# Three products of 256 columns for the feed-forward gate and up, two operands placed 64 bytes on, rotary angles in the middle of a job

## The reference

```python
h = rms_norm(x, norm2_w[l], RMS_EPS)
x = x + (jax.nn.silu(h @ w_ffn_gate[l]) * (h @ w_ffn_up[l])) @ w_ffn_down[l]   # D_FF = 5632
...
inv_freq = ROPE_THETA ** (-jnp.arange(0, QK_ROPE, 2, dtype=jnp.float32) / QK_ROPE)
ang = positions.astype(jnp.float32)[..., None] * inv_freq
cos, sin = jnp.cos(ang), jnp.sin(ang)
...
q = (_rms_norm(c_q, q_norm_g) @ w_uq)      # latents: 512 columns
kv = (_rms_norm(c_kv, kv_norm_g) @ w_ukv)  # latents: 256 columns
```

## Time and profile before

| | |
|---|---|
| timed runs, us | 2508.93, 2510.06, 2518.32 (median 2510.06) |
| the profiled execution's own time, us | 2518.45 |
| its span from first to last instruction, us | 2516.7 |
| TensorE busy | 2451.9 us, 97% |
| VectorE busy | 1524.5 us, 61% |
| ScalarE busy | 1130.1 us, 45% |
| mean granted TensorE clock | 0.991 of full speed |
| DMA | 412.26 MB, mean 164 GB/s |

### The profile page before, as it was taken

One profiled execution on the slowest core, in us unless ns is written; L12 is line 12 of the kernel. 1 busy time (PEld: TensorE's weight loads), 2 busy tenths in 40 slices (PEclk: granted clock), 3 DMA queues, 4 the chain that ended last, 5 costly groups with the idle time before them and its releaser, 6 DMA issues.

```text
span 2516.7 us, 42525 instructions
## 1 busy us (share of the span) xinstructions
PE 2451.9 (97%) x18217; PEld 2175.8 (86%) x18217; DVE 1524.5 (61%) x1902; ACT 1130.1 (45%) x1562; POOL 190.0 (8%) x198
## 2 busy tenths in 40 slices
PE   7999999999999999999999999999999999999997
PEld 7777889999888888888888899899898898999885
DVE  4999955565456556556544446745645568456555
ACT  5565545554444344344444434423444535234542
POOL 4000000002000000000000001310000151201000
PEclk9999999999999999999999999999999999999998
DMA  8454444455646565665666676424537664335465
GB/s 237 132 157 146 149 136 128 132 177 184 193 145 190 175 184 183 190 187 185 192 189 189 191 223 176 118 86 114 164 109 235 177 212 134 87 103 150 127 200 167
DMA packets 259404, 412.26 MB, mean 164 GB/s; under 512 B 53072, under 2 KB 74064, under 8 KB 258704
## 3 DMA queue, kind: packets, MB, share of 16 engines
q1 hardware_dynamic: 254496, 395.57, 52.3%
q0 software_dynamic: 4400, 13.89, 2.0%
q10 hardware_dynamic: 320, 0.08, 0.0%
HBM read 403.17 MB, written 6.30 MB: 163 GB/s over the span
## 4 chain that ended last, share of the span: by engine, by line
PE 91%; DVE 6%; ACT 2%; issue 1%; DMA 0%; ACTq 0%; SPq 0%; DVEq 0%
PE bank L568 90%; DVE wp_hl L1081 2%; ACT wp_hl L1755 1%; PE bank L780 0%; DMA xt<-x 0%; DVE r_a L1581 0%; DVE rsd L1227 0%; DVE nsd L1494 0%; DVE r_kb L1583 0%; ACT L1755 0%; PE bank L674 0%; DVE xr L1748 0%; DVE xr L1746 0%; DVE sqr L1237 0%; PE bank L859 0%
## 5 line engine op out<-in xcount | busy, mean ns | idle before, releaser
L568 PE MATMUL bank<-XX_hl,wp_hl 128*128 128x256 f32 (+1 forms) x10112 | 1436.9, 302 | 11.9 <-DVE wp_hl L1081 10.8
L1081 DVE TENSOR_TENSOR wp_hl<-raw,wp_hl 128x1024 fp32r<-128x1024 f32 x740 | 920.2, 1251 | 838.7 <-ACT wp_hl L1755 838.2
L568 PEld LDWEIGHTS bank<-XX_hl,wp_hl 128*128 128x128 f32 x10112 | 1324.3, 191 | 97.7 <-issue 13.9
L1755 ACT ACTIVATE wp_hl<-raw 128x1024 fp32r<-128x1024 f32 x740 | 781.4, 1059 | 1093.7 <-PE bank L568 1059.1
L568 PE MATMUL bank<-wp_hl,FF_hl 128*128 128x512 f32 x1056 | 240.4, 389 | 0.0
L568 PEld LDWEIGHTS bank<-wp_hl,FF_hl 128*128 128x128 f32 x1056 | 197.9, 188 | 41.0
L568 PE MATMUL bank<-wp_hl,XX_hl 128*128 128x512 f32 x576 | 139.0, 398 | 0.0
L568 PEld LDWEIGHTS bank<-wp_hl,XX_hl 128*128 128x128 f32 x576 | 107.5, 190 | 28.0 <-issue 5.3
L568 PE MATMUL bank<-wp_hl,MXa_hl 128*128 128x512 f32 x384 | 88.3, 389 | 0.0
L568 PE MATMUL bank<-wp_hl,MM_hl 128*128 128x512 f32 x384 | 87.4, 390 | 0.0
L568 PEld LDWEIGHTS bank<-wp_hl,MM_hl 128*128 128x128 f32 x384 | 71.9, 188 | 15.2 <-DVE wp_hl L1081 0.3
(11 more groups left out here) (434 smaller groups left out, 1937.7 us busy)
## 6 DMA issues: line engine op xcount, KB each, us to landing
raw<-w_in SPq DMA_DIRECT2D x304, 512.0 KB, 3.9
raw<-w_out SPq DMA_DIRECT2D x96, 512.0 KB, 4.4
raw<-w_ffn_gate SPq DMA_DIRECT2D x88, 512.0 KB, 4.4
raw<-w_ffn_up SPq DMA_DIRECT2D x88, 512.0 KB, 4.4
raw<-w_ffn_down SPq DMA_DIRECT2D x88, 512.0 KB, 3.8
raw<-w_proj_attn SPq DMA_DIRECT2D x16, 512.0 KB, 3.8
raw<-w_proj_ssm SPq DMA_DIRECT2D x16, 512.0 KB, 3.6
raw<-w_glu SPq DMA_DIRECT2D x8, 512.0 KB, 3.7
```

What stands on the lines that cost most here:

```text
L568: return e.matmul(o, lhsT, rhs, start=start, stop=stop, skip_group_check=True)
L1081: return tt(d, src, hi, SUB)
L1755: return e.activation(o, x, func, bias=bias, scale=scale)
```

## The change

Gate and up become ordinary jobs: three products of 256 columns, two banks each, `fg` emptied by ScalarE with Silu straight from PSUM, `fu` by VectorE, which multiplies `gt` by the bank; hi and lo of `FF` are written in the same place (`evac`) and no longer a piece later. `Pair` places its two halves one after the other, as they lay before. 16 words (64 bytes) are left out ahead of `XX`, and 16 ahead of `CQ` and `CK`. The rotary angles move four steps further, behind the second piece of `fu2`.

```diff
         def __init__(self, name, n):
-            self.both = v3(place(name + "_hl", 2 * n, F32R)[:, :], 2)
-            self.h, self.l = self.both[:, 0, :], self.both[:, 1, :]
+            self.h, self.l = place(name + "_hi", n, F32R), place(name + "_lo", n, F32R)
...
     xt = v3(alloc("xt", 4096), 2)
+    at[0] += 16
     XX = Pair("XX", 4096)
...
     OWN = like_the_parts()
+    at[0] += 16
     CQ, CK = Pair("CQ", 1024), Pair("CK", 512)
...
-        add(f"fg{c}", A["w_ffn_gate"][0], [(512 * c, 512)], 16, "VVVV")
-        add(f"fu{c}", A["w_ffn_up"][0], [(512 * c, 512)], 16, "VVVV")
+        add(f"fg{c}", A["w_ffn_gate"][0], [(512 * c, 512)], 16, "AA")
+        add(f"fu{c}", A["w_ffn_up"][0], [(512 * c, 512)], 16, "VV")
...
-        j.banks = tuple(range(4 * (i % 2), 4 * (i % 2) + 4)) if j.wide else (0, 1) if i % 2 == 0 else (2, 3)
+        j.banks = (0, 1) if i % 2 == 0 else (2, 3)
...
-            elif j.wide:
-                for m in range(4):
-                    d, c = B[j.banks[m]], (512 * i + 128 * m, 512 * i + 128 * m + 128)
-                    mm(d, w.hi(*c), XX.tiles(k), first, False)
-                    last = mm(d[:, 0:256], w.lo(*c), XX.tile(k)[0], False, end)
...
-            elif n[:2] == "fg":
-                c = int(j.name[2:])
-                for m in range(4):
...
-                    e.tensor_reduce(gt[2 * (c % 2) + m // 2][:, w], sides(b[m]), AXX, ADD).then_inc(s_evV, 1)
             elif n[:2] == "fu":
                 c = int(j.name[2:])
                 g = [gt[2 * (c % 2) + i] for i in range(2)]
-                for m in range(4):
...
-                    e.tensor_reduce(sqr[m // 2][:, w], sides(b[m]), AXX, ADD).then_inc(s_evV, 1)
+                e.wait_ge(s_evA, NA[f"fg{c}"])
                 for i in range(2):
-                    e.wait_ge(s_evV, j.freed[2 * i + 1][1])
-                    e.wait_ge(*FGA("s", 2 * c + i))
-                    tt(g[i], g[i], sqr[i], MUL).then_inc(FUV.made("m", 2 * c + i), 1)
+                    tt(g[i], g[i], b[i], MUL).then_inc(s_evV, 1)
+                for i in range(2):
+                    m = 2 * c + i
+                    e.wait_ge(*FSA("h", m))
+                    lo(FF.lo(512 * m, 512 * m + 512), g[i], FF.hi_f(512 * m, 512 * m + 512)).then_inc(FSV.made("l", m), 1)
...
         main(at.until("fg2"))
+        main(at.go(4))
...
             elif n[:2] == "fg":
                 c = int(j.name[2:])
                 for i in range(2):
-                    e.wait_ge(s_evV, j.freed[2 * i + 1][1])
-                    act(gt[2 * (c % 2) + i], gt[2 * (c % 2) + i], ACT.Silu).then_inc(FGA.made("s", 2 * c + i), 1)
+                    if c > 1:
+                        e.wait_ge(*FSV("l", 2 * c - 4 + i))
+                    act(gt[2 * (c % 2) + i], b[i], ACT.Silu).then_inc(s_evA, 1)
+            elif n[:2] == "fu":
+                c = int(j.name[2:])
+                for i in range(2):
+                    m = 2 * c + i
+                    e.wait_ge(s_evV, j.freed[i][1])
+                    hi(FF.hi(512 * m, 512 * m + 512), gt[2 * (c % 2) + i]).then_inc(FSA.made("h", m), 1)
```

More of the change, by code:

```diff
@@ L86, in __init__ @@
         self.name, self.W, self.pieces, self.KT = name, W, pieces, KT
-        self.home, self.tokens, self.first, self.wide = home, tokens, first, len(home) == 4
+        self.home, self.tokens, self.first = home, tokens, first
 class Pace:
@@ L195, in tile @@
             return self.hi(256 * k, 256 * k + 256), self.lo(256 * k, 256 * k + 256)
-        def tiles(self, k):
-            return self.both[:, :, 256 * k:256 * k + 256]
     cst = alloc("cst", NCONST)
@@ L465, in program @@
     GSP, MSA, MSV = marks("m_p", "a"), marks("m_hi", "h"), marks("m_lo", "l")
-    FGA, FUV, FSA, FSV = marks("f_gate", "s"), marks("f_prod", "m"), marks("f_hi", "h"), marks("f_lo", "l")
+    FSA, FSV = marks("f_hi", "h"), marks("f_lo", "l")
     ROV, ROA = marks("ang_v", "c", "f", "n1", "n2", "c1", "c2", "c3", "s", "m"), marks("ang_a", "sin", "abs", "cos")
@@ L503, in program @@
     by_chunk = lambda a: a.rearrange("p (n h s) -> p n h s", n=4, h=2)
-    sides = lambda a: a.rearrange("p (h t) -> p t h", h=2)
     blk = ctx.enter_context(nc.Block())
@@ L621, in step @@
             if first:
-                for m, b in enumerate(j.banks):
-                    bank(b, *freed(j.name, m))
+                bank(j.banks[0], *freed(j.name, 0))
+                bank(j.banks[1], *freed(j.name, 1))
             operand(j, k)
@@ L1090, in evac @@
             b = [B[x] for x in j.banks]
-            if n not in ("gs", "ga", "glu", "rg", "cg", "mg0", "mg1"):
+            if n not in ("gs", "ga", "glu", "rg", "cg", "mg0", "mg1") and n[:2] != "fg":
                 e.wait_ge(*over(j.name))
@@ L1123, in evac @@
                     tt(x, x, b[i], ADD).then_inc(s_evV, 1)
-            elif n[:2] == "fg":
-                c = int(j.name[2:])
-                for m in range(4):
-                    if c > 1 and m % 2 == 0:
-                        e.wait_ge(*FSV("l", 2 * c - 4 + m // 2))
-                    w = slice(256 * (m % 2), 256 * (m % 2) + 256)
-                    e.tensor_reduce(gt[2 * (c % 2) + m // 2][:, w], sides(b[m]), AXX, ADD).then_inc(s_evV, 1)
             elif n[:2] == "fu":
@@ L1133, in evac @@
                 g = [gt[2 * (c % 2) + i] for i in range(2)]
-                for m in range(4):
-                    if c and m % 2 == 0:
-                        e.wait_ge(*FUV("m", 2 * c - 2 + m // 2))
-                    w = slice(256 * (m % 2), 256 * (m % 2) + 256)
-                    e.tensor_reduce(sqr[m // 2][:, w], sides(b[m]), AXX, ADD).then_inc(s_evV, 1)
-                for i in range(2):
-                    e.wait_ge(s_evV, j.freed[2 * i + 1][1])
-                    e.wait_ge(*FGA("s", 2 * c + i))
-                    tt(g[i], g[i], sqr[i], MUL).then_inc(FUV.made("m", 2 * c + i), 1)
+                e.wait_ge(s_evA, NA[f"fg{c}"])
+                for i in range(2):
+                    tt(g[i], g[i], b[i], MUL).then_inc(s_evV, 1)
[3 more added lines that the diff above has]
+                    lo(FF.lo(512 * m, 512 * m + 512), g[i], FF.hi_f(512 * m, 512 * m + 512)).then_inc(FSV.made("l", m), 1)
             elif n == "misc":
@@ L1205, in rest @@
                 lo(MM.l[:, w], flat(sgs(c)), MM.hi_f(w.start, w.stop)).then_inc(MSV.made("l", c), 1)
[L1206 to L1210, removed]
-                    lo(FF.lo(512 * m, 512 * m + 512), gt[2 * (c % 2) + i], FF.hi_f(512 * m, 512 * m + 512)).then_inc(FSV.made("l", m), 1)
         def main(steps):
@@ L1800, in evac @@
             b = [B[x] for x in j.banks]
-            if n not in ("pa", "ps", "wo", "fd", "rk", "rv", "rr", "ch", "cb") and n[:2] not in ("fg", "fu", "xo"):
+            if n not in ("pa", "ps", "wo", "fd", "rk", "rv", "rr", "ch", "cb") and n[:2] not in ("fu", "xo"):
                 e.wait_ge(*over(j.name))
@@ L1871, in rest @@
                 hi(MM.hi(1024 * c, 1024 * c + 1024), flat(sgs(c))).then_inc(MSA.made("h", c), 1)
-            elif name[:2] == "fu":
-                c = int(name[2:])
-                for i in range(2):
-                    m = 2 * c + i
-                    e.wait_ge(*FUV("m", m))
-                    hi(FF.hi(512 * m, 512 * m + 512), gt[2 * (c % 2) + i]).then_inc(FSA.made("h", m), 1)
         def main(steps):
```

## The result

The changed kernel takes 2523.74 us in the median of nine runs (2521.79 to 2526.16), the kernel before 2515.91 us in nine runs of the same group (2508.93 to 2518.82). The ratio is 1.0042, 95% interval 1.003 to 1.0054: slower by 0.4%, under the 0.5% that was taken as the bound of no change. (The quotient of the two medians alone is 1.0031; the runs of before lie in two groups, so their median hangs on how many fall in each.) The forecast was 2523 us. The profiled execution's own time is 2523.74 us, 5.3 us above that of before; the forecast sum made it 6.0.

The account below looks back on a forecast made before the run. TensorE, busy 97% of the span, was taken as the bound. Profiled 2518.45 us with +11.8 and -5.8 gave 2524.5, and a fast-pace run 2523.0; it predicted 2523 us, own range 2518 to 2528 (chance 0.50), overall 2504 to 2532.

Parts of the forecast that it names:

- Step 1: Gate and up jobs: three products at 120.0 ns replace each pair of 346.7 or 353.2 ns, +11.8 us.
- Step 2: Rotary chain four steps later: TensorE's stall falls from 3.32 to 0.6 us and the low clock goes, -5.8 us.
- step 3: Bank emptying in gate and up jobs: 88 VectorE reductions go, TensorE doesn't wait at job ends, 0 us.
- Step 4: SBUF places: normed x keeps its distance from the parts, only `CQ` and `CK` move; 0, with 1.4 us either way.
- Rival B: Narrow products: the shift quickens the stream by 3.3 ns each, -40 us, 2483 us; chance 0.16.
- rival A: Timed runs before: the profiled execution is longer only because it is profiled, so 2516 us; chance 0.17.
- Rival C: Shift or new order harms: products slower by 3.3 ns, 2563 or 2537 us, or `fu` cover lost, 2534; chance 0.11.
- Rival D: Rotary chain: the stall stays as long, -5.8 becomes -0.3, so 2529 us; chance 0.06.

Follow-up runs that it names:

- experiment 2: Changed kernel without the moved rotary chain and without the 16-word shifts, so three products and new bank emptying alone: 2524.53 us, ratio 1.0037.
- experiment 3: Changed kernel with the 16 words behind the normed x instead of ahead, so it really lies 64 bytes off the weight parts' place: 2478.67 us, ratio 0.9863.
- experiment 8: Kernel before, wide jobs and places kept, with the rotary chain cut into four slices: 2506.24 us, ratio 0.9965; its profiled execution took 2513.72 us.
- experiment 1: Kernel before with only the rotary chain moved four steps later: 2507.02 us, ratio 0.9973; its profiled execution took 2506.85 us.
- experiment 9: Changed kernel with the rotary chain in four slices and only the normed x's hi part 16 words off the parts' place: 2513.21 us, ratio 0.9994.
- experiment 4: Kernel before, wide jobs kept, with the rotary chain four steps later and 16 words behind the normed x: 2496.05 us, ratio 0.9923.
- experiment 6: Changed kernel with the normed x 8 words (32 bytes) off the weight parts' place: 2513.98 us, ratio 0.9992.

## Why the prediction was right, and where it was not

**Step 1, three products for two: right, in size too.** 120.0 ns a product, and the 22 jobs, with the stall in them, grew by 6.0 us net, 512.6 against 506.6. That the whole profiled execution came out within 1 us of the sum is in part luck: the clock fell near 358 us before and not after, and that and the differences behind the jobs happened to leave 0.7 us.

**Step 2, the rotary chain: the right size by the wrong cause.** It said 0.6 us of standing, no low clock, and that this was the doing of the move. 0.63 us and 1.00 came, but experiment 2 has the same 0.6 us without the move. The working itself held the reason: it took the four reductions out of the chain's way, and step 1's new bank emptying takes them out wherever the chain stands. In the case where the move would have mattered, the wide jobs, it left 1.80 us, since it doesn't clear the splits that the reductions delay. Counting step 3 as nothing and step 2 as -5.8 us was an error of attribution that the sum can't show. That the number held is luck of a kind: the other edit, on which it wasn't put, gave the same amount.

**Step 3, bank emptying: right on cover.** No idle time of TensorE at a job's end.

**Step 4, the places: right about what the edit does, wrong on what place does.** The distance of the normed x stayed 12288 words, and its pace 120.0 ns. The latents moved and gained 2 ns a product, 0.8 us, within the 1.4 that were allowed; but a product under 118 ns was named as a sign of being wrong, with `CQ` and `CK` by name, and theirs, 117.8 ns in the mean, is just under it. But "place costs nothing", my reading of four operands that all lay in step, was no evidence on an operand that doesn't, and experiment 3 turned it over: 45 us. Rival B had this mechanism, with 40 us, and its condition, that the distance changes, was the right one: the change doesn't meet it. The Trainium skill's sentence on separate read ports ("TensorE: Matmul & The Clock Gate", Step-by-step: what each phase is for), by which streaming and weight load leave each other alone, is hard to square with these runs: 113.3 to 120.0 ns for the same product by the distance of its operands. The Trainium skill's 2.5 ns beside the columns ("TensorE: Matmul & The Clock Gate", Back-to-back issue gap) is said of an isolated matmul, and the prediction held it against a stream in which each product has a weight load; in these streams the least is 113.3 - 106.7 = 6.6 ns. (106.7 ns are 256 columns, one in each cycle of 2.4 GHz; here a product of 512 columns in the down projection takes 226.8 ns, 106.8 more than one of 256.)

**The two readings of the median.** Runs of before fall into two groups, near 2510 and 2518 us, and the profiled executions put a pace to each group: 353.2 ns with 2518.45 us and 2513.72 us (experiment 8), 346.6 with 2506.85 (experiment 1). So rival A, that profiling lengthens the run, falls, and the loss against before depends on which pace its runs take: 2523.7 is 13.7 us above the first median and 7.8 above the one of nine runs. I had expected the changed kernel's own runs in one group; they spread over 4.4 us, with 120.0 ns in the one that was profiled. The clock goes with that spread: the four runs from 2521.79 to 2522.35 us have a mean granted clock of 0.994, the five from 2523.74 to 2526.16 us 0.992 or 0.993, and 0.001 of the execution is 2.5 us. It does not go with the two groups of before, where 2509.99 and 2516.42 us both have 0.992.

Rivals C and D didn't come: no product grew, and the stall did not stay.

**What stays open.** What sets the pace at which a stream settles, and why 16 and 48 words have a pace of 113.3 ns that 8, 24 and 32 don't show, was not settled. A shift of the normed x moves it against the `raw` buffers too, which DMA fills and ScalarE and VectorE read. Their work doesn't set the 120.0 ns, though: in the changed kernel the starts between 860 and 1180 us are 120 ns apart one and all, whether DMA moves 369 GB/s or nothing (the last two numbers are the DMA engines' busy share and GB/s):

```profile
1001.50:1002.00 0.50, 0.50 (x7) 0.50 (x6) 0.25 (x2) 0.33 (x1) 0.00 (x0) 1.00 0.98 369
1003.00:1003.50 0.50, 0.50 (x6) 0.50 (x5) 0.09 (x1) 0.50 (x1) 0.00 (x0) 1.00 0.00 0
```

That leaves TensorE's own two reads, of x and of the weights, as the likeliest to meet, since the pace hangs on their distance and on no absolute place tried. The runs show the dependence and not the mechanism; experiment 9 shows only that it isn't confined to one product in gate and up.

## What to carry to other kernels

When two edits of one change remove the same work from an engine's queue, run each alone before giving either the credit: here the move of the rotary chain was worth nothing beside the edit that took the reductions away. An offset meant to separate two buffers must stand between them; placed ahead of both it shifts both, as the allocator's arithmetic shows without a chip. And when a stream of like instructions has a constant surplus per instruction, measure it at several operand distances before taking it as the instruction's own: 64 bytes between the two operands were worth 45 us of 2524 here, and decided which of two ways of cutting the products was the better. Look at more than one stretch of the trace for that, and on both sides of a stall, since one distance can have two paces.

## What the runs showed of the hardware that was not expected

- A stream of float32r products of 128 rows by 256 columns, each with its own weight load, at 2.4 GHz: one every 120.0 ns where the buffers of the two operands start a multiple of 2048 bytes apart (the tiles that one product reads then lie a multiple of 512 bytes apart, and all of them take 120.0 ns), 118.3 at 32 bytes off, 117.3 or 118.7 at 96, 118.7 or 120.0 at 128, and 113.3 or 117.8 at 64 and at 192.
- Paces persist. The pair of 512 and 256 columns keeps 346.7 or 353.2 ns over hundreds of microseconds. In three profiled executions the pace changed at the idle time of TensorE at the rotary chain, twice to the slower (before, experiment 3) and once to the faster (32 words); in five it stayed through one (experiments 1, 2, 4 and 6, the changed kernel). Times in two groups about 8 us apart fit a pace that differs from execution to execution of one program.
- The length of an idle time of TensorE doesn't decide alone whether the clock falls. Those of 0.63 and 1.80 us at the rotary chain left the granted clock at 1.00; the one of 3.32 us in the earlier trace rows went with the fall to the lower level, 1.2 GHz; and one of 1.73 us near 358 us went with 0.80 from 355 to 372 us in the kernel before and with 1.00 in the changed one.
